# First two query strips computed as one pair with a Strassen unit on a quarter of their depth, in a two-layer encoder kernel

## The reference, cut to what matters

```python
kv = rms_norm(h, g) @ w_kv          # 2048 x 4096: K (rotary), V
q = (rms_norm(h, g2) @ w_q)         # 2048 x 2048, rotary on 32 of each 128
a = softmax(q0 k0) - lam * softmax(q1 k1)
o = rms_norm(a @ v) @ w_o           # then residual, MLP, final norm
```

## Time and profile before

| | us |
|---|---|
| median of 3 runs | 1786.91 (1786.77 to 1787.15) |
| profiled execution, its own time | 1786.59 |
| span of its instructions | 1784.8 |
| PE busy | 1775.7 (99%) |
| DVE busy | 1512.6 (85%) |
| ACT busy | 1215.3 (68%) |
| DMA queue, share of 16 engines | 57.5% |
| granted TensorE clock, mean | 0.999 |

### The profile page before, as it was taken

The page is one execution under the profiler, slowest core; times in us unless marked ns, Lnnn a source line. Parts: engine busy times, 40 slices in busy tenths (PEclk is TensorE's granted clock), DMA queues, the critical chain, the costliest instruction groups (busy, mean ns, idle before and its releaser), DMA issues.

```text
span 1784.8 us, 21406 instructions
## 1 busy us (share of the span) xinstructions
PE 1775.7 (99%) x8100; PEld 1473.4 (83%) x8100; DVE 1512.6 (85%) x1540; ACT 1215.3 (68%) x1513; POOL 12.1 (1%) x17
## 2 busy tenths in 40 slices
PE   9999999999999999999999999999999999999998
PEld 7888888888888888888888888888888888888886
DVE  7888999999898987877757776889998999998986
ACT  7677777777777775755445555677777777767772
POOL 0000000000000000000000000000000000000000
PEclk9999999999999999999999999999999999999999
DMA  8555657565656565555564446465656565655572
GB/s 312 179 181 179 237 176 242 176 207 189 214 189 229 193 202 198 161 194 198 185 212 159 132 158 212 165 213 172 206 189 220 177 237 187 217 189 189 198 248 96
DMA packets 178663, 348.83 MB, mean 195 GB/s; under 512 B 10624, under 2 KB 10752, under 8 KB 178176
## 3 DMA queue, kind: packets, MB, share of 16 engines
q1 hardware_dynamic: 177984, 346.02, 57.5%
q10 hardware_dynamic: 576, 1.44, 0.2%
HBM read 345.32 MB, written 2.10 MB: 195 GB/s over the span
## 4 chain that ended last, share of the span: by engine, by line
PE 98%; issue 0%; DMA 0%; DVE 0%; POOL 0%; SPq 0%; DVEq 0%; POOLq 0%; ACT 0%; ACTq 0%
PE bank L1673 15%; PE bank L1675 15%; PE bank L1674 15%; PE bank L1679 13%; PE bank L1681 13%; PE bank L1680 13%; PE bank L1638 4%; PE bank L1640 4%; PE bank L1639 4%; PE bank L1708 2%; PE bank L1665 1%; DMA h<-in_x 0%; PE bank L2041 0%; PE bank L1914 0%; PE bank L2040 0%
## 5 line engine op out<-in xcount | busy, mean ns | idle before, releaser
L1037 DVE TENSOR_TENSOR w_lo<-raw,w_hi 128x1024 fp32r<-128x1024 f32 x392 | 469.5, 1220 | 4.2 <-ACT w_hi L591 3.3
L597 ACT ACTIVATE w_hi<-raw 128x1024 fp32r<-128x1024 f32 x224 | 236.9, 1058 | 224.7 <-DVE raw L1053 147.5
L1679 PE MATMUL bank<-w_hi,u_hi_a 128*128 128x512 f32 x896 | 349.1, 390 | 0.0
L1681 PE MATMUL bank<-w_hi,u_lo_a 128*128 128x512 f32 x896 | 348.7, 389 | 0.0
L1680 PE MATMUL bank<-w_lo,u_hi_a 128*128 128x512 f32 x896 | 348.6, 389 | 0.0
L1673 PE MATMUL bank<-w_hi,mix_hi 128*128 128x512 f32 x828 | 323.9, 391 | 0.0
L1675 PE MATMUL bank<-w_hi,mix_lo 128*128 128x512 f32 x828 | 322.3, 389 | 0.0
L1674 PE MATMUL bank<-w_lo,mix_hi 128*128 128x512 f32 x828 | 322.2, 389 | 0.0
L1031 DVE TENSOR_TENSOR w_lo<-arena,w_hi 128x2048 fp32r<-128x2048 f32 x110 | 248.3, 2287 | 49.0 <-ACT w_hi L585 49.0
L585 ACT ACTIVATE w_hi<-arena 128x2048 fp32r<-128x2048 f32 x110 | 207.7, 1908 | 20.9 <-PE bank L1675 17.9
L591 ACT ACTIVATE w_hi<-raw 128x1024 fp32r<-128x1024 f32 x168 | 174.2, 1053 | 41.7 <-DMA raw<-in_w_mlp_in 37.3
(11 more groups left out here) (228 smaller groups left out, 2643.4 us busy)
## 6 DMA issues: line engine op xcount, KB each, us to landing
raw<-in_w_mlp_in SPq DMA_DIRECT2D x240, 512.0 KB, 5.2
arena<-in_w_mlp_out SPq DMA_DIRECT2D x240, 512.0 KB, 6.5
raw<-in_w_kv SPq DMA_DIRECT2D x64, 512.0 KB, 4.5
raw<-in_w_q SPq DMA_DIRECT2D x32, 512.0 KB, 5.4
raw<-in_w_o SPq DMA_DIRECT2D x32, 512.0 KB, 4.6
arena<-in_w_mlp_in SPq DMA_DIRECT2D x16, 512.0 KB, 6.3
raw<-in_w_mlp_out SPq DMA_DIRECT2D x16, 512.0 KB, 4.8
raw<-in_pool_w SPq DMA_DIRECT2D x4, 512.0 KB, 9.9
```

Of the source, the lines that this page charges most:

```text
L597: nc.scalar.activation(w_hi[:, slot], raw_half[half][:, i], ACT.Copy).then_inc(hi_ready, 1)
L1037: nc.vector.tensor_tensor(w_lo[:, slot], raw_half[half][:, i], w_hi[:, slot].bitcast(F32), ALU.subtract).then_inc(lo_ready, 1)
L1679: nc.tensor.matmul(bank[:], hi, w_hi[:, slot, kk, :], start=False, stop=False, skip_group_check=True)
L1681: return nc.tensor.matmul(bank[:], lo, w_hi[:, slot, kk, :], start=False, stop=False, skip_group_check=True)
```

## The change

The first two Q strips become a fifth pair (j = 4 = `PAIRS`). They take 19 pieces instead of 16, so all that follows moves by 3 slots (`MLP_AT`). The second strip of the pair is gathered in `o_n` (`second_strip`) and brought to `kq` by DVE (`q_second`) instead of ACT. The token sums are made anew from the query input (`q_rows`, `q_sum`, `q_mix_hi`, `q_mix_lo`), in the queue between pair 3 and the new pair. The first head pair's turn of queries, first scores and second scores, which lay in strip t = 1, come after steps 14, 16 and 17 of the pair. Strip t = 2 and all after it keep their order.

```diff
+        def kv_summed_at(j):
+            return 5 + 2 * (j - 1) + (5 if j == PAIRS else 0)
+
+        def second_strip(j, tb):
+            return o_n[:, tb] if j == PAIRS else v[:, tb, j * SW:(j + 1) * SW]
...
-            for j in range(1, PAIRS):
+            for j in range(1, PAIRS + 1):
                 load_kv_pair(j)
-            for t in range(PAIRS):
+            for t in range(2, PAIRS):
                 load_strip(S_Q + t, in_rows(q_view[0], t * SW))
...
+                kv_hi(j + 1, range(1))
+                kv_last_copies(j)
+                kv_hi(j + 1, range(1, 3))
+                if j + 1 == PAIRS:
+                    act.wait_ge(kv_summed, kv_summed_at(PAIRS))
+                    nc.scalar.activation(q_mix_hi[:], q_sum, ACT.Copy).then_inc(kv_mixed, 1)
+                kv_hi(j + 1, range(3, 6))
...
+            kv_hi(PAIRS, range(6, 8))
+            kv_hi(PAIRS, range(8, 13))
+            kv_first_copies(PAIRS)
+            kv_hi(PAIRS, range(13, 15))
+            kv_copy(PAIRS, 10, X[0], kq[:, 1], 1)
+            kv_hi(PAIRS, range(15, 19))
+            kv_last_copies(PAIRS)
+            split(S_Q + 2, 0)
+            split(S_Q + 2, 1)
+            split(S_Q + 2, 2)
+            exps(0, (0, 1))
...
+            split(S_Q + 2, 3)
+            exps(0, (2, 3))
...
+                kv_lo(j + 1, range(2))
+                v_second(j)
+                if j + 1 == PAIRS:
+                    kv_sums(q_rows, q_sum, b_hi0, b_lo0, kv_summed_at(PAIRS) - 5)
+                    kv_lo(PAIRS, range(2, 3))
+                    kv_low(q_mix_lo, q_sum, q_mix_hi, 3)
+                    kv_lo(PAIRS, range(3, 5))
...
+                k_turned(j)
+                kv_lo(j + 1, range(5, 6))
+                v_rest(j)
...
+            kv_lo(PAIRS, range(6, 15))
+            k_first(PAIRS)
+            kv_lo(PAIRS, range(15, 16))
+            k_second(PAIRS)
+            rope(PAIRS)
+            kv_lo(PAIRS, range(16, 19))
+            v_second(PAIRS)
+            split(S_Q + 2, 0)
+            q_turned(0)
+            split(S_Q + 2, 1)
+            split(S_Q + 2, 2, (0,))
+            maxima(0, 0)
+            lambda_dots()
+            split(S_Q + 2, 2, (1,))
+            split(S_Q + 2, 3, (0,))
+            maxima(0, 1)
+            q_second()
+            rope(PAIRS + 1)
+            negative_lambda()
+            differences(0)
+            split(S_Q + 2, 3, (1,))
...
                 for n in range(2, HALVES):
                     kv_plain(j, n + 11, n, PAIR[1], (False, n == 2), n == HALVES - 1)
+                    if j == PAIRS and n == 3:
+                        attention(1, 0)
+                    elif j == PAIRS and n == 5:
+                        pe.wait_ge(kv_copied, 4 * j)
+                        pe.wait_ge(kv_summed, kv_summed_at(j) + 2)
+                        attention(1, 1)
+                    elif j == PAIRS and n == 6:
+                        attention(1, 2)
```

More of the change, by code:

```diff
@@ L221, in trunk @@
         kv_sum = place(2048, 4, 2, P)
+        q_rows = place(BACK, 4, SEQ)
+        q_sum = place(9728, 4, 2, P)
         squares = place(BACK, TB, D)
@@ L1520, in sub_scale, with q_turned @@
                     last.then_inc(o_done, 1)
-            for t in range(2 * PAIRS):
+            def q_turned(u):
+                for b in range(2):
+                    dve.wait_ge(t_ready, 2 * R_ATT[("q", u)] + b + 1)
+                    nc.vector.tensor_copy(q_t[:, 2 * b:2 * b + 2, :], T[b][:].rearrange("p (c t) -> p c t", c=2)).then_inc(t_taken, 1)
+            kv_lo(PAIRS, range(6, 15))
[19 more added lines that the diff above has]
+            split(S_Q + 2, 3, (1,))
+            for t in range(2, 2 * PAIRS):
                 s = S_Q + t
@@ L1537, in _ @@
                         plain_lot(1, g)
-                    if t == 0 and g == 2:
-                        negative_lambda()
                     if g == 0 and 0 <= t - 1 < PAIRS:
-                        for b in range(2):
-                            dve.wait_ge(t_ready, 2 * R_ATT[("q", t - 1)] + b + 1)
-                            nc.vector.tensor_copy(q_t[:, 2 * b:2 * b + 2, :], T[b][:].rearrange("p (c t) -> p c t", c=2)).then_inc(t_taken, 1)
+                        q_turned(t - 1)
                     if g == 1 and 0 <= t - 3 < PAIRS:
@@ L1978, in kv_plain @@
             def kv_plain(j, step, n, banks, begin, end):
+                tile = b_tile if j == PAIRS else a_tile
                 at = strip_at(S_KV + 2 * j)
@@ L2003, in kv_strassen_pair @@
             def kv_strassen_pair(j):
[L2005 to L2008 removed]
+                hi, lo, mix_hi, mix_lo = (b_hi0, b_lo0, q_mix_hi, q_mix_lo) if j == PAIRS else (a_hi0, a_lo0, kv_mix_hi, kv_mix_lo)
+                a11 = lambda kk: (hi[:, kk, 0:P], lo[:, kk, 0:P])
+                a12 = lambda kk: (hi[:, 2 + kk, 0:P], lo[:, 2 + kk, 0:P])
+                a22 = lambda kk: (hi[:, 2 + kk, P:], lo[:, 2 + kk, P:])
+                s4, s1, s2, s3 = (lambda kk, i=i: (mix_hi[:, i, kk, :], mix_lo[:, i, kk, :]) for i in range(4))
                 pe.wait_ge(kq_out, j * TB)
@@ L2088, in attention @@
                         nc.tensor.matmul(X[hh][:, VD:2 * VD], attn_t[:, hh, 2 * P:3 * P], v[:, 1, cols], start=False, stop=True).then_inc(pv_done, 1)
-            for t in range(2 * PAIRS):
+            kv_strassen_pair(PAIRS)
+            for t in range(2, 2 * PAIRS):
                 s = S_Q + t
-                if t == 1:
-                    pe.wait_ge(v_done, PAIRS)
-                elif t < PAIRS:
-                    pe.wait_ge(kq_out, (PAIRS + t - 1 if t else PAIRS) * TB)
+                if t < PAIRS:
+                    pe.wait_ge(kq_out, (PAIRS + t - 1) * TB)
                 for g in range(NG):
```

111 lines of the change are left out of this document (49 added, 62 removed).

## The result

The changed kernel takes 1789.67 us (median of 18 executions, 1788.85 to 1791.94); the kernel before, in the same comparison, 1786.91 (18 executions, 1786.48 to 1787.46). The ratio over all executions is 1.0017, 95% interval 1.0011 to 1.0024. The medians differ by 2.8 us: slower beyond noise, but within the 0.2% that the prediction calls no change. The spread grew from 1.0 to 3.1 us. The profiled execution is the longest of the 18, 1791.94, so its waits are some 2 us more than the median's.

A forecast was written before the change was run, and what follows sets the result against it. PE was taken as the bound, full with products and interruptions, so every wait is lost in full. Six fewer products (-1.36) and four waits (1.0, 1.6, 0.6, 1.1) gave +2.9 on 1786.91: 1789.8 us, range 1785.5 to 1793.6.

The forecast's parts named there:

- The gain: In the new pair, six products fewer on PE at 0.2274 us each: 1.36 us less, the whole gain possible.
- DVE enters the pair late: At the pair's entry, token sums put step 6's low part at +4.5, making DVE 2.9 us later than in pair 3.
- Wait 1: Ahead of step 12, PE waits 1.0 us for ACT's copy of X[0], behind the load and rounding of step 14.
- Wait 2: Ahead of the first scores, PE waits 1.6 us for DVE's copied turned queries, behind a low part needing a late load.
- Wait 3: Ahead of the second scores, PE waits 0.6 us behind three low parts and the first maxima, whatever the loads do.
- Wait 4: Ahead of `turn_differences`, PE waits 1.1 us for DVE's `differences`, with no load in it.
- The sum: Over the kernel, -1.36 and waits of 1.0, 1.6, 0.6 and 1.1 make +2.9 us.
- Costed at nothing: Lambda steps, `q_second` and three extra pieces lie beside PE's work, no cost but their part ahead of `turn_differences`.
- swallowed lateness: Rival: in the pair, fast loads and tighter DVE hand-overs remove waits, -1.36 to +0.4, 1785.6 to 1787.3 us; chance 0.18.
- Long loads: Rival: slow loads ahead of step 12 and the first scores, waits above 6.2 us; 1793.6 at 6.5 a load; chance 0.17.
- the price of 2 us for each 1 us: Each 1 us more per load ahead of step 12 and the first scores costs 2 us, as both waits grow.
- wait at the turn: Rival: with DVE over 1.7 us later, PE waits at the turn instead of the scores, 1790 to 1791; within the 0.60.

The follow-up runs named there:

- run 10: As run 9, with ACT's second exponentials ahead of the rounding of the third Q strip's piece 7: 1785.99 us, ratio 0.9997.
- run 11: As run 10, with DVE's copy of the first head's turned queries one low part earlier: 1786.07 us, ratio 0.9995.
- run 6: As run 4, with copies of the second queries and turned attention weights behind one low part instead of five; sums at the entry: 1791.39 us, ratio 1.0024.
- run 4: Changed kernel with more low parts behind DVE's copied queries, maxima and differences, and two roundings behind ACT's exponentials: 1791.51 us, ratio 1.0024.
- run 8: Changed kernel with each of the two sets of maxima one low part earlier, token sums still at the entry: 1787.79 us, ratio 1.0007.
- run 2: Changed kernel with ACT's copies after steps 6 and 9 put ahead of the roundings of steps 11 and 14: 1790.58 us, ratio 1.0022.
- run 1: Changed kernel without the token sums, their low part and rounding; the unit multiplies plain token halves, so values differ: 1787.51 us, ratio 1.0005.
- run 3: Changed kernel with the token sums moved from the entry into three gaps of the weight-sum chain where DVE waits for ACT: 1787.42 us, ratio 1.0005.
- run 9: As run 3, with each of the two sets of maxima one low part earlier: 1786.51 us, ratio 0.9998.
- run 7: Changed kernel with the pair's weights read from w_kv instead of w_q, so queries are not the reference's: 1788.96 us, ratio 1.0012.
- run 12: Changed kernel with the token sums' addition of the rows made three times over at the entry: 1793.23 us, ratio 1.0037.

## Why the prediction was right, and where its steps were off

The forecast was 1789.8, the result 1789.67. It is right in mechanism: four waits of PE made by DVE's queue and its loads (the first of them in two parts, at steps 9 and 12), against six products less. That the sum fits to 0.1 us is luck. In the profiled execution its single terms are off by up to 2 us, with both signs, and other executions lie up to 2.3 us away from the median.

**The gain, -1.36.** 8094 products, at 0.227 us where no wait stands between them. Runs 10 and 11, with hardly a wait left, are 0.7 to 0.8 below the kernel before; their waits of 0.4 and 0.8 are about what is missing. From the first to the last product with weights, run 10's profile takes 0.93 us less than that of the kernel before with one wait of 0.38.

**DVE enters the pair late.** Forecast: step 6's low part at +4.5 after the pair's start. It came at +5.1. The order and the lengths of what stands there were right; `v_second` itself began 0.75 later than forecast, since the low part ahead of it waited 2.3 us for a rounding, and this for a load that took 7.5.

**Wait 1, forecast 1.0, profiled 2.9 (with refill 3.5; refill is what a wait costs beyond its idle time).** This is the term that was furthest off, for two reasons. First, I set the first weight sum three low parts behind, at +7.9, and looked at the load of its fourth tile, which "may just be in time at 4.7 us". The sum came at +9.9: beside the late entry it was step 8's own load that counted, 6.1 us, and step 8's low part waited 1.1 for its rounding. Secondly I looked only at step 12. Step 9 needs a copy that ACT's queue has behind the rounding of step 12, and that rounding depends on the same ring; with step 11's low end at +21.7 instead of +19.7, it was late as well. From there the step holds: the load of step 14 took 4.46 (forecast 4.3).

How late the first weight sum comes is a matter of the execution. Three more kernels have the changed kernel's queues up to step 12: runs 6, 4 and 8. In their profiles it came at +9.5, +9.1 and +7.7, and the waits at steps 9 and 12 were 2.1, 1.7 and 0.5. The three loads issued 14 to 17 us ahead of the pair took 7.5 to 7.7 us in the changed kernel, 6.9 to 7.2 in run 6, 6.5 to 6.7 in run 4 and 6.0 to 6.3 in run 8. So the forecast of +7.9 is what run 8 shows, and the changed kernel's profile is its longest execution. Run 8 (its pair begins at 895.15):

```profile
902.89 1.22 DVE L1404 TENSOR_TENSOR raw<-raw 128x1024 f32<-128x1024 f32 x1
...
PE bank L1730 <- ACT arena L933: 0.5, 1, 0.5
```

**Wait 2, forecast 1.6, profiled 0.8.** Here the mechanism was right, and the size follows from the load. PE was due some 2.5 us later than I had it, but the load was issued 2.4 us later as well (929.72, that is +34.3 instead of +31.9), as both hang on the same ring. It took 4.05 us (landed at 933.77) instead of the 4.88 that I had, and the wait is shorter by that. Run 2 shows that DVE's copies set the first scores: with the waits of steps 9 and 12 gone, this one is 2.3.

**Wait 3, forecast 0.6, profiled 1.2.** It needs no load, I said; but DVE's low parts ahead of the maxima did wait for one, as the row at 938.11 shows, 0.8 us behind the copies: the load was issued at 930.86 and landed at 937.00. So "whatever the loads do" was wrong. In run 1 the wait is gone: the three loads there took 5.3 to 5.7 us, where those of run 3 took 5.6 to 6.1 and those of the changed kernel 5.8 to 6.3. In run 3 it is there (1.0) though PE has no wait ahead of it. The order makes it, as run 8 shows by taking it away with one low part less ahead; how much of it the loads make, no run shows by itself.

**Wait 4, forecast 1.1, profiled 0.6.** Right in kind and nearly in size: counted from the second scores, the differences ended at 11.2 us (forecast 11.4) and PE was due at 10.6 (forecast 10.3). Of the four it is the one that run 1 leaves, 0.6. Runs 8 and 9 take it to 0.2, though the same low parts stand ahead of it: in run 8 DVE no longer waits 1.4 us for a rounding between the two sets of maxima.

**The sum.** Waits of 4.3 were forecast. The profiled execution shows 5.5 (6.5 with refill), but took 2.3 more than the median; the median says 2.76 + 1.36 = 4.1.

**Costed at nothing.** The MLPs cost nothing in the profile: both windows are 300.00 of 300.00. The lambda steps and `q_second` stand only in the chain ahead of wait 4, as forecast.

**The rivals.** The swallowed lateness did not come. By the Trainium skill, "DMA: Bandwidth & Descriptors", section "Anatomy of one DMA", 512 KB take an estimated 3.2 us on the GpSimd path; these loads are issued by SP, and no load of the entry was as short, not even those of the K/V weights in run 7, at 3.6 to 5.6. Long loads came in part, 6.1 and 5.1 at the entry, but not at the two loads to which I gave the price of 2 us for each 1 us: these took 4.46 and 4.05. So that price is not tested. (By my terms the result passes +3.6 at 4.9 us a load, not at 5.1.) Run 12 shows another one: 2.0 us of lateness of DVE at the entry made the first wait 2.0 longer and cost 3.6 in all, with the slower clock in it. PE did not wait at the turn, except in run 2.

What stays open is the spread of 3.1 us. The loads of the same place differ by up to 1.5 us between profiles with the same queues, and the first weight sum by 2.2 with them, which could make it. But only one execution of each kernel was profiled, so it is not shown, nor why the loads differ.

## What to carry to other kernels

The total of an engine's work says little when its order is the limit: DVE is idle for 11.6 of the pair's 51.87 us, and 4 us of sums at the wrong place cost 2.0 to 2.3. Look for gaps in the queue where the engine waits for another anyway, and put the new work there (run 3), before reordering what others depend on. When a step is moved ahead of others, move it past one, look, and stop: one low part less ahead of the maxima won 1.8 to 1.9 us; with three low parts behind the differences, and the copies behind those, a wait of 3.1 came back. Profile more than one execution where the spread has grown: the longest one showed waits of 2.9 us where another with the same queues showed 0.5.

## What the runs showed of the hardware

- A wait of PE cost more than its idle time: the idle times of 1.45 and 1.48 us cost 1.72 and 1.75, by the pitches around them.
- An idle time of 3.5 us brought PE's granted clock from 1.00 to 0.50, and twelve products took 2.4 us more in all; behind one of 3.1 us in run 4 the clock stayed at 1.00.
- Around the pair of the changed kernel a load of 512 KB took 3.8 to 7.7 us: 7.7 for two issued at 880.16 and 881.43 with two and three others in flight, 3.8 for one issued at 913.64 alone. The number in flight is not all of it: one issued at 930.86 with one other took 6.1.
